# A mixture-of-experts scatter-add on one Trainium2 core: two accumulators in DRAM instead of one, and VectorE's wait for a scatter moved to where it scales the outputs

## The reference

```python
def _swiglu(x, w1, w3, w2):
    return (jax.nn.silu(x @ w1) * (x @ w3)) @ w2

def block_fn(acc, inp):                       # one block: 128 rows of one expert
    rows, wts, e = inp
    xb = x_pad[rows]
    yb = _swiglu(xb, w1[e], w3[e], w2[e]) * wts[:, None]
    return acc.at[rows].add(yb), None
...
routed, _ = lax.scan(block_fn, acc0, ...)     # top 8 of 64 experts for each of 1024 tokens
return routed[:N] + _swiglu(x2d, sw1, sw3, sw2)
...
x = _layernorm(DN_ALPHA * x + ffn, ln2_g[l], ln2_b[l])
```

## Time and profile before

| | |
|---|---|
| median of 3 runs | 2719.61 us |
| the profiled execution | 2750.55 us |
| its span in the profile | 2747.8 us |
| busy: PE, DVE, ACT, POOL | 86%, 48%, 31%, 22% |
| mean granted clock of PE | 0.928 of full speed |
| DMA: mean rate | 142 GB/s over the span |

### The profile page before, as it was taken

One profiled execution on the slowest core, in us unless ns is written; L12 is line 12 of the kernel. 1 busy time (PEld: TensorE's weight loads), 2 busy tenths in 40 slices (PEclk: granted clock), 3 DMA queues, 4 the chain that ended last, 5 costly groups with the idle time before them and its releaser, 6 DMA issues.

```text
span 2747.8 us, 36372 instructions
## 1 busy us (share of the span) xinstructions
PE 2375.9 (86%) x8956; PEld 1541.4 (56%) x8957; DVE 1306.7 (48%) x2144; ACT 844.0 (31%) x1049; POOL 598.9 (22%) x403
## 2 busy tenths in 40 slices
PE   9976878999989999999635888989989989889992
PEld 3454554555545444445323667777767777677771
DVE  6275712243334111114461466665676766565665
ACT  1032111111111110001111456454555645455442
POOL 1000001120202000000036433333333333333333
PEclk9997969999999999999866999999999999999996
DMA  3001001100000111143212589797898988778864
GB/s 143 31 31 24 9 0 69 35 27 31 0 23 23 34 42 38 34 187 133 96 62 46 156 274 313 239 312 229 283 311 239 328 265 257 247 239 277 276 163 160
DMA packets 85449, 390.65 MB, mean 142 GB/s; under 512 B 15361, under 2 KB 15617, under 8 KB 59394
## 3 DMA queue, kind: packets, MB, share of 16 engines
q1 hardware_dynamic: 51522, 274.21, 26.3%
q0 software_dynamic: 33888, 115.95, 17.7%
HBM read 318.47 MB, written 70.47 MB: 142 GB/s over the span
## 4 chain that ended last, share of the span: by engine, by line
PE 39%; DMA 18%; issue 8%; DVE 3%; DVEq 2%; ACT 2%; another core or an unknown queue 1%; POOL 0%; ACTq 0%; POOLq 0%; SPq 0%
DMA ffn_rows<-yo,sx 17%; PE ps L611 14%; PE ps L1265 10%; PE ps L1273 5%; PE ps L566 4%; PE ps L1127 2%; DVEq L375 1%; PE ps L605 1%; PE ps L1301 1%; DVE yo L923 1%; ACT xgT L693 1%; PE ps L639 1%; PE ps L584 1%; ACT wts L681 1%
## 5 line engine op out<-in xcount | busy, mean ns | idle before, releaser
L611 PE MATMUL ps<-wts,xgT 128*128 x2616 | 652.8, 405 | 28.0 <-issue 22.9
L611 PEld LDWEIGHTS ps<-wts,xgT 128*128 128x128 f32 x2616 | 494.3, 192 | 163.0 <-issue 52.5
L870 DVE TENSOR_TENSOR wts<-wts (+1 forms) x195 | 443.9, 2289 | 120.5 <-issue 88.6
L611 PE MATMUL ps<-wts,hTs 128*128 x1296 | 362.8, 431 | 82.9 <-DVE hTs L905 58.5
L611 PEld LDWEIGHTS ps<-wts,hTs 128*128 128x128 f32 x1296 | 256.4, 205 | 151.5 <-issue 97.8
L1265 PE MATMUL ps<-xT,ring 128*128 128x512 f32 x768 | 334.7, 593 | 0.0
L1127 PE MATMUL ps<-xT,ring 128*128 128x512 f32 x704 | 311.4, 599 | 6.1 <-DMA ring<-in_w_in 6.1
L529 POOL DMA_INDIRECT ffn_rows<-yo,sx x108 | 216.9, 2009 | 387.8 <-DVE yo L923 191.9
L512 POOL DMA_INDIRECT xg<-x_rows,ix x112 | 200.5, 1790 | 378.5 <-DVE ix L894 366.0
L681 ACT ACTIVATE wts<-wts (+1 forms) x130 | 241.8, 1908 | 75.2 <-issue 75.2
L1265 PEld LDWEIGHTS ps<-xT,ring 128*128 128x128 f32 x768 | 145.2, 190 | 178.9 <-issue 178.9
(11 more groups left out here) (359 smaller groups left out, 2290.1 us busy)
## 6 DMA issues: line engine op xcount, KB each, us to landing
wts<-in_experts SPq DMA_DIRECT2D x195, 1024.0 KB
ring<-in_w_in SPq DMA_DIRECT2D x52, 512.0 KB, 3.3
bring<-in_w_branch SPq DMA_DIRECT2D x24, 256.0 KB, 2.6
xT<-in_xT SPq DMA_DIRECT2D x4, 1024.0 KB, 9.2
wout<-in_w_out SPq DMA_DIRECT2D x1, 4096.0 KB, 12.4
N<-in_x SPq DMA_DIRECT2D x8, 512.0 KB, 3.3
x_rows<-N SPq DMA_DIRECT2D x8, 512.0 KB, 2.6
ffn_rows<-sig SPq DMA_DIRECT2D x8, 512.0 KB, 2.8
```

What stands on the lines that cost most here:

```text
L611: ins = mm(o, left(x), slot_cols(s, w, slice(c0, c0 + HALF)), start=first and n == 0, stop=last and n == 2)
L870: tt(w, w.bitcast(F32), hi, ALU.subtract).then_inc(done, 1)
```

## The change

The accumulator becomes two tensors, `accd[0]` for even blocks and `accd[1]` for odd ones, each with its own semaphore `e_sc[k]`. A scatter waits for the one two before it. `accd[1]` starts as zeros: POOL stores `sig` nine times more (128 x 1024 each), and ACT's first write of `sig` waits for these as well. In `block_step` the wait for the scatter and the copies to `sx` and `wx` move from the start of the step to just ahead of the output's scaling. At the end SP loads both tensors (`fr` and `fs`), and DVE adds them.

```diff
@@ -37,6 +37,7 @@
 NBT = NBMAX + 4
 TRASH = P
 NROW = T + TRASH
+SC0 = (16 * 2, 16 * (KD + 1))
 ALPHA = 2.0 ** 0.25
 LN_EPS, RMS_EPS = 1e-5, 1e-6
 BIG = 1e30
@@ -118,7 +119,7 @@
 
 
         x1d = nc.dram_tensor("x1_rows", [NROW, D], F32, kind="Internal").ap()
-        accd = nc.dram_tensor("ffn_rows", [NROW, D], F32, kind="Internal").ap()
+        accd = [nc.dram_tensor(f"ffn_rows{i}", [NROW, D], F32, kind="Internal").ap() for i in range(2)]
         slotd = nc.dram_tensor("slot_table", [P * NBT, 2], I32, kind="Internal").ap()
         blockd = nc.dram_tensor("block_table", [2 * P, 4], I32, kind="Internal").ap()
 
@@ -353,7 +356,7 @@
         e_wx = sem("row_weight_ready")
         e_ya = sem("output_half_act")
         e_yd = sem("output_half_dve")
-        e_sc = sem("rows_adding")
+        e_sc = [sem(f"rows_adding{i}") for i in range(2)]
         e_ix = sem("gather_rows_named")
         f_in = [sem(f"ffn_rows_loaded{i}") for i in range(KD)]
         f_var = sem("ffn_variance")
@@ -465,9 +468,12 @@
             announce(w_o, 63 % 3, (63 // 3 + 1) * 16, s_wo2)
             announce(w_o, 64 % 3, (64 // 3 + 1) * 16, s_wo2)
             n = counts(sp)
-            sp.wait_ge(e_sc, n * 32 + 32)
+            for k in range(2):
+                sp.wait_ge(e_sc[k], n * 16 + SC0[k])
+                sp.sem_inc(sp_go, 1)
             for t in range(KD):
-                sp.dma_start(fr[:, t], accd[t * P:(t + 1) * P, :]).then_inc(f_in[t], 16)
+                for rows, part in zip((fr, fs), accd):
+                    sp.dma_start(rows[:, t], part[t * P:(t + 1) * P, :]).then_inc(f_in[t], 16)
             for t in range(KD):
                 store_out(sp, t)
             sp.wait_ge(f_out, 16 * KD)
@@ -476,7 +482,7 @@
             sp.wait_ge(s_x1, t + 1)
             sp.dma_start(x1d[t * P:(t + 1) * P, :], x1[:, t % 2]).then_inc(s_x1s[t % 2], 16)
             sp.wait_ge(s_xa, t + 1)
-            sp.dma_start(accd[t * P:(t + 1) * P, :], sig[:, :, :].rearrange("p a b -> p (a b)")).then_inc(s_xas, 16)
+            sp.dma_start(accd[0][t * P:(t + 1) * P, :], sig[:, :, :].rearrange("p a b -> p (a b)")).then_inc(s_xas, 16)
 
         def store_out(sp, t):
             sp.wait_ge(f_y, t + 1)
@@ -488,7 +494,9 @@
             g.memset(sig[:], 0.0).then_inc(s_z, 1)
             pool.wait_ge(s_z, 1)
             for r in (slice(0, TRASH // 2), slice(TRASH // 2, TRASH)):
-                pool.dma_start(accd[T:NROW][r], sig[r, :, :].rearrange("p a b -> p (a b)")).then_inc(e_sc, 16)
+                pool.dma_start(accd[0][T:NROW][r], sig[r, :, :].rearrange("p a b -> p (a b)")).then_inc(e_sc[0], 16)
+            for t in range(KD + 1):
+                pool.dma_start(accd[1][t * P:(t + 1) * P, :], sig[:, :, :].rearrange("p a b -> p (a b)")).then_inc(e_sc[1], 16)
 
             pool.wait_ge(s_lg, KD)
             g.iota(slt[:, 0:SHB, 0:1], pattern=[[P, SHB], [0, 1]], base=0, channel_multiplier=1).then_inc(s_slt0, 1)
@@ -504,7 +512,8 @@
             for k in range(2):
                 pool.wait_ge(s_x1s[k], 8 * KD)
             pool.wait_ge(s_zd, 16)
-            pool.wait_ge(e_sc, 32)
+            for k in range(2):
+                pool.wait_ge(e_sc[k], SC0[k])
             pool.wait_ge(s_xas, 16 * KD)
 
             def gather(k):
@@ -520,14 +529,15 @@
                 ch.link(g.tensor_copy(ix[:, c % 2:c % 2 + 1], slt[:, c, 0:1]))
                 gather(c % 2)
 
-            def add_rows(b, u):
-
-                pool.wait_ge(e_sc, b * 16 + 32)
+            def add_rows(i, u):
+
+                b = i * 2 + u
+                pool.wait_ge(e_sc[u], i * 16 + SC0[u])
                 pool.wait_ge(e_ya, b + (1 + ONE))
                 pool.wait_ge(e_yd, b + (1 + ONE))
                 pool.sem_inc(p_go, 1)
-                g.indirect_dma_start(out=accd, out_offset=bass.IndirectOffsetOnAxis(ap=sx[:, u:u + 1], axis=0),
-                                     in_=yo[:, u, :], in_offset=None, compute_op=ALU.add).then_inc(e_sc, 16)
+                g.indirect_dma_start(out=accd[u], out_offset=bass.IndirectOffsetOnAxis(ap=sx[:, u:u + 1], axis=0),
+                                     in_=yo[:, u, :], in_offset=None, compute_op=ALU.add).then_inc(e_sc[u], 16)
 
             for c in range(4):
                 named_gather(c)
@@ -539,16 +549,15 @@
                 if b + 4 == SHB:
                     pool.wait_ge(s_slt, 16)
                 named_gather(b + 4)
-                add_rows(b, b % 2)
+                add_rows(b // 2, b % 2)
             n = counts(pool)
             with pool.Fori(SHB // 2, n) as i:
                 for u in range(2):
-                    b = i * 2 + u
                     pool.wait_ge(e_ix, i * 2 + (u + 1 - SHB))
                     pool.wait_ge(e_T, i * 2 + (u + 3))
                     pool.sem_inc(p_go, 1)
                     gather(u)
-                    add_rows(b, u)
+                    add_rows(i, u)
 
             for t in range(KD):
                 pool.wait_ge(f_g, t + 1)
@@ -657,7 +666,8 @@
                 if t >= 1:
                     act.wait_ge(s_x1, t)
                     act.wait_ge(s_zd, 16)
-                    act.wait_ge(e_sc, 32)
+                    for k in range(2):
+                        act.wait_ge(e_sc[k], SC0[k])
                     if t >= 2:
                         act.wait_ge(s_xas, 16 * (t - 1))
                     A(sig[:, :, :].rearrange("p a b -> p (a b)"), x1[:, (t - 1) % 2], ACT.Copy, scale=ALPHA).then_inc(s_xa, 1)
@@ -896,10 +906,6 @@
             def block_step(i, u, named):
 
                 b = i * 2 + u
-                dve.wait_ge(e_sc, i * 32 + (16 * u + 16))
-                dve.sem_inc(d_go, 1)
-                V.tensor_copy(sx[:, u:u + 1], slt[:, bass.ds(b, 1), 0:1].rearrange("p o w -> p (o w)")).then_inc(e_wx, 1)
-                V.tensor_copy(wx[:, u:u + 1], sltf[:, bass.ds(b, 1), 1:2].rearrange("p o w -> p (o w)")).then_inc(e_wx, 1)
                 dve.wait_ge(e_hTe, i * 2 + (u + 1) + ONE)
                 h_ = lambda x: hTs[:, x].rearrange("p a b -> p (a b)")
                 tt(h_(0), ps[4][:, 0:2 * P], h_(1).bitcast(F32), ALU.subtract).then_inc(e_hTl, 1)
@@ -918,6 +924,10 @@
                 o, s, first = block_entry(dve, i * 2 + (u + 1))
                 with dve.If(first > 0):
                     split2(o, s)
+                dve.wait_ge(e_sc[u], i * 16 + SC0[u])
+                dve.sem_inc(d_go, 1)
+                V.tensor_copy(sx[:, u:u + 1], slt[:, bass.ds(b, 1), 0:1].rearrange("p o w -> p (o w)")).then_inc(e_wx, 1)
+                V.tensor_copy(wx[:, u:u + 1], sltf[:, bass.ds(b, 1), 1:2].rearrange("p o w -> p (o w)")).then_inc(e_wx, 1)
                 dve.wait_ge(e_Y, i * 2 + (u + 1) + ONE)
                 dve.wait_ge(e_wx, i * 4 + (2 * u + 2))
                 ts(yo[:, u, HALF:D], ps[7][:], wx[:, u:u + 1], None, ALU.mult).then_inc(e_yd, 1)
@@ -940,9 +950,10 @@
 
             for t in range(KD + 2):
                 if t < KD:
-                    dve.wait_ge(f_in[t], 16)
+                    dve.wait_ge(f_in[t], 32)
                     if t >= 2:
                         dve.wait_ge(f_n, t - 1)
+                    L(tt(fr[:, t], fr[:, t], fs[:, t], ALU.add))
                     for h in range(2):
                         N(V.bn_stats(fst[:, t % 2, h], fr[:, t, h * HALF:(h + 1) * HALF]))
                     ch.wait()
```

More of the change, by code:

```diff
@@ L207, in build @@
         fr = sbx(lay_f, "fr", [P, KD, D])
+        fs = sbx(lay_f, "fs", [P, KD, D])
         lay_f.close()
@@ L270, in build @@
         d_go = sem("dve_waited")
+        sp_go = sem("sp_waited")
         w_full = [sem(f"w_full{i}") for i in range(6)]
```

## The result

The changed kernel takes 2806.37 us, the median of 4 runs (2804.98 to 2809.77), against 2719.93 (2713.70 to 2730.28, 4 runs) for the kernel before beside it: a ratio of 1.031, 95% interval 1.028 to 1.033. The forecast was 2819 us, slower by 99; it is slower by 86.

What follows compares the result with a forecast made beforehand. It took PE to pace steps without waits (9.85 us), with DVE stalled 130.5 us for scatters. Loop +71, zeros +8 and end +20 made +99 on the median 2719.6: 2819 us, range 2765 to 2875.

Steps and rivals of the forecast that it cites:

- part 1: Block loop: with two accumulators and a later wait, both kinds of wait for scatters (DVE's 130.5 us) would be gone.
- part 2: Block loop: late `wx` makes ACT and DVE take turns; 100 steps take 1195 us against 1124, +71 (+20 to +158).
- B to A: Loop step splitting only w1/w3's second half, after one splitting only w2: 11.7 us each, 36 steps, together 421.
- A to B: Loop step splitting only w2, after one splitting only w1/w3's second half: 10.2 us each, 21 steps, together 214.
- kind C: Loop steps splitting both w2 and w1/w3's second half: 28 of 100, ACT's piece 8.7 us, steps expected at 13 to 15.
- part 3: Output projection: nine stores of zeros (4.7 MB) delay ACT's first write of `sig`; +8 us, ends 3 and 12.
- half of the 16: Output projection: ACT's lateness of up to 16 us, less a half projection, was taken as 8 us.
- part 4: Second layernorm: DVE's adds held up beside POOL's, tiles of 6.6 us instead of 3.57, doubled loads; +20 us, 12 if not held.
- ACT not held by `wx`: Rival for the loop: ACT isn't tied to DVE's tail and the stall's end shows; 2694 us, chance 0.07.
- Full DMA engines: Rival for the loop: DMA engines pace it anyway at 11.24 us a step, only fixed costs stay; 2748 us, chance 0.08.
- Late gathers: Rival for the loop: gathers queue behind two scatters and PE waits for rows, 0.3 us a step; 2850 us, chance 0.05.
- PE's clock: Rival for the loop: idle PE makes hidden products slow more often; 2906 us, or 2862 at half the excess; chance 0.18.

Runs made afterwards that it cites:

- the second execution of before: The kernel before, unchanged, profiled a second time: 2719.93 us, its 100 loop steps 1119.0 us.
- the third group: Third set of runs on one chip, changed kernel unchanged and with the end's add moved, beside the kernel before: 2832.24 and 2822.66 us against 2748.5.
- the kernel that runs its 100 steps in 1009 us: Changed kernel with `wx` written early, right behind the low part of `hTs`, and ACT waiting for the scatter itself; two accumulators: 2666.68 us, ratio 0.975.

## Why the prediction was right, point by point

**The waits for scatters (part 1)** are gone, as it said, and worth nothing. The move alone ends DVE's, as the run with one accumulator showed. My later expectation, that two accumulators with early copies would cut them to 40 us, was refuted by the run with the copies left early.

**The moved copies (part 2)** carry the result. From one end of the rows' low part to the next, in the changed kernel:

| step kinds | count | forecast, us | measured, us |
|---|---|---|---|
| B to A | 36 (35 measured) | 11.7 | 11.54 |
| A to B | 21 | 10.2 | 9.91 |
| A to C | 15 | 12.7 | 12.23 |
| C to B | 15 | 11.6 | 11.91 |
| C to C | 13 | 15.0 | 14.45 |
| all 100 | | 1195 | 1174.9 |

The order of size is right and each is within 0.6 us; the sum is 20 us too high: 7 us each from A to C and C to C, 6 each from B to A and A to B, less 5 from C to B. In the steps now of kind C I had carried ACT's longest piece as 8.7 us; in the one that begins with the `yo` of 2093.70 it is 8.4 (ended at 2102.07), some 0.3 of the 0.5 us that they are too dear. A to B came at PE's own pace: hidden products start at 2070.43 and 2080.28, 9.85 us apart, as in the earlier trace rows, and take 5.86 us, not 7.39. The 7 us that I had put on there for a slow PE (21 times 0.35) were nearly all absent: 9.91 against 9.85.

Against the second execution of before (1119.0) the loop loses 56 us, against the one that I read (1124.2) 51; the forecast was 71. That term was mis-sized; its mechanism is shown twice, by the run with the move alone and by the run that unties `wx`.

**The zeros (part 3)** cost 14.5 us (154.7 for 140.2 from the projection's first product to the last logits), where I took 8 with an upper end at 12. The start of ACT's first write, "near 1254 if they end last", was 1253.48: they ended last, 24 us (median) after issue, and ACT was 15.2 us late by the two profiles' times, 17.0 counted from the projection's start. What failed is the choice of half of the 16. Less the half projection of 7 us that the prediction itself names they are 9, and PE waited 10.9. A second cost wasn't in it: behind the wait PE's products took 3.6 us more, at the lower clock.

The Trainium skill ("DMA: Bandwidth & Descriptors", Queues, rings and completion order) has an engine take turns between its queues packet by packet. The trace agrees: from 1225 to 1245 us of the changed kernel the two queues moved the same number of packets (packets, MB, share of 16 engines' time):

```profile
q1 hardware_dynamic: 770, 5.59, 66.4%
q0 software_dynamic: 770, 2.82, 34.5%
```

What the prediction added to the rule was wrong: half of the packets isn't half of the rate. The packets of POOL's queue (q0) were half as large, 4096 bytes each beside 8192 on SP's, which loads the weights, apart from some of 4 bytes in both, so the zeros got a third of the bytes and ended at 1253, not near 1245.

**The end (part 4)** was +20 and measured +20.0 against the second execution, +20.5 against the first. That the add would be held, and by how much, came out as reasoned. The add beside POOL's took 3.27 us, and the tile 6.42 against 6.6. By the Trainium skill ("SBUF — State Buffer", SBUF: two separate sides) a VectorE instruction with two inputs in SBUF and a GpSimd instruction that reads SBUF shut each other out: whichever starts first holds the shared ports for its whole instruction. The trace agrees: 1.22 us alone, 3.27 when started 0.15 us behind an add of 2.34 (2.34 - 0.15 + 1.22 = 3.41), and moving the add away gave 9.6 us.

**The sum** came out 13 us too high: the loop was 15 us too dear against the second execution of before, the zeros 6.5 too cheap, and the stretches that the forecast left alone came out 4 us shorter. That the loop's error and the zeros' partly cancel is luck. "The difference carries over" took the median as base, which was right: 22 of the 31 us by which the profiled execution lay above it are the long form of the stretch ahead of the loop, and the timed runs of both kernels in the first measurement lay near their profiles with the short form (2719.93 and 2805.28). A sum against the 2750.6 alone would have come out 31 us higher. That the difference carries over is borne out in the third group, where it is 84 us (2832.2 less 2748.5).

**The signs.** Four of those named came as said: no wait of DVE or POOL for a scatter, `yo` waiting for `wx` in every step, the low part of the rows right behind ACT, adds of 3.27 us beside POOL's. Steps of kind C took 14.5 us from `yo` to `yo` (in the table's measure 12.2 behind an A and 14.5 behind a C), and the DMA share from 1988 to 2037 us was 0.90, at the edge of what was named. "Wrong in size if B steps come out at 9.85" came true for those behind an A (9.91).

**The rivals.** ACT not held by `wx`: refuted, 102 waits. Full DMA engines: refuted, both by the longer loop and by the kernel that runs its 100 steps in 1009 us at a share of 1.03. Late gathers: no such wait in the loop. PE's clock: its condition came true in part, its price didn't. The granted clock from 1550 to 2700 us was 0.95 (0.97 in the profile that the prediction read, 0.95 in the second of before), but 28 of the changed kernel's 101 hidden products took 7.2 to 8.6 us, against 4 of 100 in either execution of before. All but one are in or right behind a step of kind C, not in the A to B steps for which the prediction feared it. One of them, at a granted clock of 0.77, and ACT's waits for hidden products from 1550 to 2750 us:

```profile
2104.07 7.39 PE L620 MATMUL ps<-wts,xgT 128*128 x24 [1.93 <-issue]
```

```profile
ACT si L710 <- PE ps L620: 7.8, 4, 4.0
```

Together they are 48 us longer than at 5.86 us each, but ACT and DVE set the pace of those steps, and ACT waited for PE there only 4 times.

## What to carry to other kernels

When a wait or a copy is moved to a later place in an engine's order, look first at who else waits for what it writes: one small copy behind three long subtractions tied ACT to DVE's tail, and the two took turns instead of overlapping. Give each consumer its own condition at its own place (here `wx` early, `sx` and the scatter's wait late), which was worth 85 us in the loop, where a second accumulator alone was worth 21 there and cost 34 at the ends. Price a second buffer at both ends, setting it up and joining it, and put both where the engines involved have nothing else to do.

## What the hardware showed that I had not expected

- Nine stores of 512 KB, issued by POOL at a time when SP's loads of weights fill the DMA engines, landed 24 us after issue (median). The two queues moved 770 packets each from 1225 to 1245 us, but 2.82 MB against 5.59.
- A scatter-add of 128 rows of 4 KB took 13 us from issue to landing beside dense loads of weights, with no other scatter in its way; so a wait for it one step later shows in steps of about 10 us.
- The DMA engines at a share of 1.03 gave 372 to 375 GB/s to the faster kernel, with PE busy 19 of 20 us. A share of 1.01 and 351 GB/s in the kernel before had looked like a bound, and it was not one.
- One stretch of 104 to 107 us, ahead of the loop, takes 126.6 to 129.5 us in seven of twelve profiled executions, with PE idle on "issue" for 38 to 45 us of it in place of 1. One profile of a kernel is not enough to call such a stretch its own, or a disturbance.
